# Order of ScalarE's and VectorE's work in the recurrence layer of a seven-block model on one core

## The reference

```python
def rglru_block(xn, w_in, conv_w, conv_b, w_a, b_a, w_x, b_x, lam, w_out):
    u = xn @ w_in
    xb, gate = jnp.split(u, 2, axis=-1)
    xc = lax.conv_general_dilated(xb, conv_w, ...) + conv_b          # 4 taps along time
    r = sigmoid(einsum('bsgi,gij->bsgj', xg, w_a) + b_a)             # 8 blocks of 256
    i_gate = sigmoid(einsum('bsgi,gij->bsgj', xg, w_x) + b_x)
    log_a = -8 * r * softplus(-lam)
    a, bt = exp(log_a), sqrt(-expm1(2 * log_a)) * (i_gate * xc)
    h_t = a_t * h_(t-1) + bt_t                                       # scan along time
    return (h * silu(gate)) @ w_out
```

## Time and profile before

| What | Before |
|---|---|
| Median of 3 runs | 3548.23 us (3548.18 to 3550.38) |
| The profiled execution's own time | 3549.42 us |
| Its span in the profile | 3547.6 us |
| TensorE busy (matmuls) | 3447.0 us, 97% |
| VectorE busy | 2783.1 us, 78% |
| ScalarE busy | 1987.5 us, 56% |
| POOL busy | 587.2 us, 17% |
| Mean granted TensorE clock | 0.995 of full |

### The profile page before, as it was taken

One profiled execution on the slowest core, in us unless ns is written; L12 is line 12 of the kernel. 1 busy time (PEld: TensorE's weight loads), 2 busy tenths in 40 slices (PEclk: granted clock), 3 DMA queues, 4 the chain that ended last, 5 costly groups with the idle time before them and its releaser, 6 DMA issues.

```text
span 3547.6 us, 68240 instructions
## 1 busy us (share of the span) xinstructions
PE 3447.0 (97%) x27858; PEld 3381.8 (95%) x27858; DVE 2783.1 (78%) x4529; ACT 1987.5 (56%) x3204; POOL 587.2 (17%) x546
## 2 busy tenths in 40 slices
PE   7999999999999999999999999999999998999997
PEld 7999999999999998999999999999999998999997
DVE  7788888577797887877888887898989867666665
ACT  6555546566547676565555546665656746434344
POOL 2111112111113011131111112231313300000000
PEclk9999999999999999999999999999999999999999
DMA  6555556444465444655555565556464543555552
GB/s 239 217 197 219 217 227 231 176 155 179 165 251 203 172 169 173 267 185 218 201 221 202 208 262 180 178 175 230 171 233 169 186 169 146 210 189 199 204 190 107
DMA packets 113688, 699.61 MB, mean 197 GB/s; under 512 B 13216, under 2 KB 29792, under 8 KB 31456
## 3 DMA queue, kind: packets, MB, share of 16 engines
q1 hardware_dynamic: 104128, 685.14, 52.2%
q10 hardware_dynamic: 8784, 8.46, 1.0%
q0 software_dynamic: 464, 1.64, 0.1%
HBM read 684.64 MB, written 2.16 MB: 194 GB/s over the span
## 4 chain that ended last, share of the span: by engine, by line
PE 49%; DVE 13%; ACT 6%; issue 2%; DMA 1%; POOL 1%; DVEq 0%; SPq 0%; POOLq 0%; ACTq 0%
PE g L446 15%; PE g L448 15%; PE g L447 15%; DVE w_lo L1594 4%; ACT w_hi L1026 2%; DMA w_raw<-in_slots 1%; POOL scratch L2409 1%; DVE vec L2095 1%; DVE rstd L2095 1%; PE turn_bank L485 1%; DVE scratch L1659 1%; DVE scratch L2121 0%; DVE scratch L2129 0%; PE norm_bank L459 0%; DVE h L2225 0%
## 5 line engine op out<-in xcount | busy, mean ns | idle before, releaser
L1594 DVE TENSOR_TENSOR w_lo<-w_raw,w_hi 128x1024 fp32r<-128x1024 f32 x1088 | 1337.0, 1232 | 433.9 <-ACT w_hi L1026 423.1
L1026 ACT ACTIVATE w_hi<-w_raw 128x1024 fp32r<-128x1024 f32 x1088 | 1129.6, 1053 | 873.2 <-PE g L448 761.7
L446 PE MATMUL g<-p_hi,w_hi 128*128 128x256 f32 x4576 | 1318.0, 288 | 36.4 <-DVE w_lo L1594 23.2
L448 PE MATMUL g<-p_hi,w_lo 128*128 128x256 f32 x4576 | 1296.2, 283 | 0.0
L447 PE MATMUL g<-p_lo,w_hi 128*128 128x256 f32 x4576 | 1296.2, 283 | 0.0
L446 PE MATMUL g<-q_hi,w_hi 128*128 128x256 f32 x3408 | 980.0, 288 | 5.7 <-DVE w_lo L1594 2.2
L448 PE MATMUL g<-q_hi,w_lo 128*128 128x256 f32 x3408 | 964.0, 283 | 0.0
L447 PE MATMUL g<-q_lo,w_hi 128*128 128x256 f32 x3408 | 963.8, 283 | 0.0
L446 PEld LDWEIGHTS g<-p_hi,w_hi 128*128 128x128 f32 x4576 | 879.1, 192 | 46.1 <-DVE w_lo L1594 32.7
L447 PEld LDWEIGHTS g<-p_lo,w_hi 128*128 128x128 f32 x4576 | 879.3, 192 | 1.4
L448 PEld LDWEIGHTS g<-p_hi,w_lo 128*128 128x128 f32 x4576 | 879.0, 192 | 0.0
(11 more groups left out here) (445 smaller groups left out, 3929.2 us busy)
## 6 DMA issues: line engine op xcount, KB each, us to landing
w_raw<-in_slots SPq DMA_DIRECT2D x640, 1024.0 KB, 4.9
scratch<-scratch SPq DMA_DIRECT2D x128, 64.0 KB, 4.9
scratch<-s_rows ACTq DMA_DIRECT2D x16, 256.0 KB, 3.4
con<-s_rows ACTq DMA_DIRECT2D x16, 256.0 KB, 5.1
h<-in_x SPq DMA_DIRECT2D x4, 512.0 KB, 6.2
out_h<-h SPq DMA_DIRECT2D x4, 512.0 KB, 2.6
sq<-in_p POOLq DMA_DIRECT2D x4, 256.0 KB, 3.0
con<-in_consts SPq DMA_DIRECT2D x1, 832.0 KB, 10.7
```

The source lines that it names most:

```text
L446: pe.matmul(g, wh, hi[:, k], start=n == 0, stop=False)
L448: last = pe.matmul(g, wl, hi[:, k], start=False, stop=n == len(ks) - 1)
L1026: act.activation(w_hi[k % SPLIT][:, cols], raw[MAIN_AT[k] % RAW][:, cols], ACT.Copy).then_inc(hi_ready, 1)
L1594: dve.tensor_tensor(w_lo[k % SPLIT][:, cols], raw[MAIN_AT[k] % RAW][:, cols], w_hi[k % SPLIT][:, cols], SUB).then_inc(lo_ready, 1)
```

## The change

Two things change, both in the recurrence layer. On ScalarE the block of a z slot (sigmoid of the gate tile, high part of the output tile before it, and in z12 the split of the `ple` input) moves from behind the group's chain to ahead of it; in slots without a piece of a chain nothing changes. On VectorE the four scans of a group are cut in two for groups 1, 2 and 3: the first two stay 5 slots after the group, the other two come at the end of the next slot. Group 0 keeps its four in one slot. No instruction is added or removed.

```diff
@@ -1319,6 +1319,12 @@
                 else:
                     act.wait_ge(tile_done, c.next("tile"))
                 hi_ahead(1)
+                if kind == "z":
+                    sigmoid(c_zc[n % 2], clamped, c.next("clamped"))
+                    if n:
+                        y_high(n - 1)
+                    if n == 12:
+                        split_p(layer)
                 for g in range(4):
                     if s == C_AT[g] + 1:
                         c_sigmoid(rg, 8 * g + 4)
@@ -1328,12 +1334,6 @@
                         c_decay()
                     if s == C_AT[g] + 4:
                         c_scale()
-                if kind == "z":
-                    sigmoid(c_zc[n % 2], clamped, c.next("clamped"))
-                    if n:
-                        y_high(n - 1)
-                    if n == 12:
-                        split_p(layer)
             y_high(DT - 1)
             p_slot()
             out_and_gates(layer, x, y)
@@ -2007,10 +2007,10 @@
                 last = dve.tensor_tensor(b[:, 512 * e:512 * e + 512], b[:, 512 * e:512 * e + 512], bS[e][:], MUL)
             link(last)
 
-        def c_scan(g):
-            for n in range(4):
-                last = dve.tensor_tensor_scan(xc[:, 4 * g + n], rg[:, n], ig[:, n], 0.0, MUL, ADD)
-            link(last)
+        def c_scan(g, first, last):
+            for n in range(first, last):
+                done = dve.tensor_tensor_scan(xc[:, 4 * g + n], rg[:, n], ig[:, n], 0.0, MUL, ADD)
+            link(done)
 
         def layer_c(layer, x, y):
             lam_ = vec[:, VEC["c_lambda"]:VEC["c_lambda"] + DT]
@@ -2066,7 +2066,9 @@
                         c_input_gate(g)
                     if s == C_AT[g] + 5:
                         c_scale()
-                        c_scan(g)
+                        c_scan(g, 0, 2 if g else 4)
+                    if g and s == C_AT[g] + 6:
+                        c_scan(g, 2, 4)
             finish(DT - 1)
             low(DT - 2)
             low(DT - 1)
```

## The result

The kernel after the change takes 3567.07 us, the median of 5 runs (3563.53 to 3568.04), against 3548.18 us for the kernel before in the same comparison (5 runs, 3545.65 to 3550.38). The ratio is 1.0051, with a 95% interval of 1.0040 to 1.0062: slower by some 19 us, half a percent. The forecast was 3567.4.

What follows compares the result with a forecast made beforehand. TensorE, busy 97%, bounds the kernel; in late z slots ScalarE waits for POOL's clamp. Order + 20.4 and scans - 1.2 give + 19.2 us (19.1 slot by slot): 3568.5 profiled, median 3567.4, range 3557 to 3574.

Steps and rivals of the forecast that it cites:

- The chain stands behind the clamp's wait: ScalarE, seven z slots: a group's chain would wait for POOL's clamp instead of filling that time, 20.4 us lost.
- The terms: Loss per z slot with a chain piece (13, 20, 22, 25 to 28): 2.6 to 3.2 us each, sum 20.4.
- The scans: VectorE, two of four scans one slot later: 1.2 us gained in group 3, 0 in groups 1 and 2.
- Passing on: Between the seven slots: each delay arrives in full; TensorE's slots 19 to 22 only some 2 us later.
- The earlier high part: VectorE's wait for the high part (L1309): serving it earlier frees 0, at most 0.4 us a slot.
- The clock: TensorE's gaps before slots 25 and 28 to 31: falls to the lower clock level there cost 0.
- The signs: Expected in the later profile: seven new ScalarE waits for POOL of 2.3 to 3.2 us, slots 26 to 28 longer.
- the test: TensorE's slot 32, at 1357.22 before: forecast wrong if it starts less than 15 us later.
- absorption of the early slots: ScalarE's waits for TensorE between z1 and z2 make slots 13 and 20 cost nothing: 3561 us, chance 0.08.
- Slack on TensorE all along: TensorE keeps the slack of slots 19 to 22 throughout, so the time does not change; chance 0.04.
- A lasting low clock: TensorE at the lower clock level from slot 28 to 31: some 3 us more, 3570.5 us, chance 0.08.
- the scans decide: Seven z slots wait under 0.5 us for the clamp, three scan splits win 1.22 us each: median 3544.6, chance 0.04.

Runs made afterwards that it cites:

- the order alone: ScalarE's new order (sigmoid and high part ahead of the chain) with VectorE's scans unsplit, against the kernel before: 3568.24 us, ratio 1.0057.
- the halves: Two kernels, ScalarE's new order only in slots 13, 20, 22 or only in 25 to 28, scans unsplit, against the kernel before: 3557.41 and 3558.88 us.
- the high part alone: Only the high part moved ahead of the chain, sigmoid left behind it, scans unsplit, against the kernel before: 3569.40 us, ratio 1.0059.

## Why the prediction was right

It gave 3567.4 us with a range of 3557 to 3574, and 0.92 for slower; the median is 3567.07. That the two agree to 0.3 us is luck: the interval of the ratio leaves 14 to 22 us for the loss, and the two profiled executions differ by 16.8 us in span. What carries the account is the single slots, which the traces show to a few hundredths. Going by the prediction's own steps:

- **The chain stands behind the clamp's wait, and the hole that it filled is lost.** Shown by the order alone (+20.30), the halves (9.11 + 11.17), and the high part alone (+20.46), in which another wait of the same kind does the same.
- **The terms.** Forecast 3.18, 3.18 and 3.2 for slots 13, 20 and 25: measured 3.11, 3.12 and 3.11. Forecast 2.8 for slot 22: 2.89. Forecast 2.7, 2.6 and 2.7 for slots 26 to 28: 2.70, 2.68, 2.69. Their sum is 20.30 against 20.4. A further 0.25 us comes up before the slots 20 and 25; it is the scans' (next point).
- **The scans** give 1.18 in group 3 (forecast 1.2). In groups 1 and 2 I put them at 0, and they cost 0.11 and 0.14. TensorE's gap only moved from slot 26 to 27.
- **Passing on.** It passes on in full, as forecast, and TensorE starts slots 19 to 22 by 1.93 to 2.02 us later (forecast some 2), slot 23 by 4.54. Two readings on the way were wrong, without a price. In slots 23 and 24 ScalarE is not without idle time: it waits 2.58 us for the clamp and then 4.10 for the gate reads (L1989), and the delay goes on over VectorE, whose gate reads of slot 25 come 9.37 us later. And of ScalarE's 6.6 us of waiting for TensorE only two waits, 4.8 us, lie between z1 and z2.
- **The earlier high part gives back 0.** From the start of ScalarE's first half to VectorE's (L1594) it is 1.15 us in slot 29 before (1346.52 to 1347.67) and 1.16 in slot 28 after (1356.51 to 1357.67), so nothing is won. The reading behind it was off: what happens 0.3 us ahead of T is the start of the high part. VectorE's wait for it ends 0.13 us behind T, at 1346.65, and it then still waits 0.59 for the half.
- **The clock.** I put its falls at 0, and the Trainium skill (TensorE: Matmul & The Clock Gate, "Why this matters for your kernels") warns that idle gaps between bursts of matmuls send the clock back to half. The trace agrees with it that the clock falls after gaps, of 4.5 and 5.1 us among others. Its price is nil in this place. The slot that starts at 1359.38 runs at the lower level at first, and TensorE still waits 2.71 us for the take behind it. The gaps that I forecast before slots 28 to 31 (3.4 to 5 us) came out as 3.58, 1.76, 5.06 and 2.71, because slow matmuls filled part of them.
- **The signs.** The waits of ScalarE for POOL grew in seven slots, five of them new and two lengthened, as forecast. That each would last 2.3 to 3.2 us missed two: 3.54 in slot 20, where the former 0.41 is in it, and 7.25 in slot 25, where I had not counted that the chain's wait for L1989 would merge with it. No time hangs on either. The slot times of 9.3, 10.9 and 10.5 are 9.23, 11.03 and 10.55. TensorE begins slot 32 without a gap at 1377.24, 20.0 us later than at 1357.22 and over the 15 that I had put as the test. The take that it needs was at 1376.04, so by the 0.56 us of before it could have begun at 1376.6: the last low spell holds it up by 0.6 us here, and the clamps behind show nothing of it (19.37 to 19.39).

The rivals: absorption of the early slots would have given 6.4 us less, and slots 13 and 20 cost 3.12 and 3.11 with nothing else moved but slot 22. Slack on TensorE all along would have given nothing. A lasting low clock would have added 3, and nothing of it is there. For "the scans decide" the waits would have to be under 0.5 us; the smallest new one is 2.58.

Why ScalarE can't use the hole otherwise is in its queue's order: the path in a z slot is weight half, take, clamp, sigmoid, next weight half, over three engines, and ScalarE has 2.58 us in the middle of it that only work without a wait can fill.

## What to carry to other kernels

Before moving an instruction forward in the queue of an in-order engine, look for what waits it carries and what it would be moved past: work that waits for nothing hides in another's wait if it stands ahead of it (here 2.6 to 3.1 us each time) and is paid in full behind it. If one engine's wait for another shows in every pass of a loop (here 2.58 us in the plain slots), the move that helps is the other one, back by a pass, behind work that the next pass needs anyway; here it took the time from 3548.0 to 3542.6 where the forward move took it to 3567. And a wait that one sees on a second engine (17.0 us of VectorE at L2039) is no reason to serve it sooner, as long as that engine then waits for the same first engine anyway.

## What the runs showed of the hardware that I had not expected

The same instruction on POOL has different durations. A clamp of 128x256 float32 takes 1.65 us in most z slots, and 0.84 to 0.91 when repeated right behind itself, as shown above. The kernel before has both as well, in clamps behind the layer (timeline of POOL):

```profile
1492.97 1.64 POOL L2409 TENSOR_SCALAR scratch<-scratch 128x256 f32<-128x256 f32 x1 [7.71 <-DVE scratch L1702]
1498.77 0.85 POOL L2409 TENSOR_SCALAR scratch<-scratch 128x256 f32<-128x256 f32 x1 [4.16 <-DVE scratch L1702]
...
1503.84 1.89 POOL L2409 TENSOR_SCALAR scratch<-scratch 128x256 f32<-128x256 f32 x1 [3.34 <-DVE scratch L1702]
...
1509.89 0.85 POOL L2409 TENSOR_SCALAR scratch<-scratch 128x256 f32<-128x256 f32 x1 [3.46 <-DVE scratch L1702]
```

The two-input work of VectorE next to them decides, as far as the rows go. Timeline of VectorE around the same four clamps:

```profile
1492.69 1.22 DVE L1594 TENSOR_TENSOR w_lo<-w_raw,w_hi 128x1024 fp32r<-128x1024 f32 x1
...
1498.80 1.45 DVE L1594 TENSOR_TENSOR w_lo<-w_raw,w_hi 128x1024 fp32r<-128x1024 f32 x1 [0.22 <-ACT w_hi L1026]
...
1503.80 1.23 DVE L1594 TENSOR_TENSOR w_lo<-w_raw,w_hi 128x1024 fp32r<-128x1024 f32 x1 [0.15 <-ACT w_hi L1026]
1504.94 0.62 DVE L1666 SCALAR_TENSOR_TENSOR q_lo<-h,vec,q_hi 128x256 fp32r<-128x256 f32 x1
...
1509.91 1.46 DVE L1594 TENSOR_TENSOR w_lo<-w_raw,w_hi 128x1024 fp32r<-128x1024 f32 x1 [0.21 <-ACT w_hi L1026]
```

Where the weight half (L1594, two inputs from SBUF) starts first, at 1492.69 and 1503.80, the clamp lasts until 0.8 us after its end (1492.69 + 1.14 to the next start = 1493.83, and the clamp ends at 1494.61; 1504.94 and 1505.73). Where the clamp starts first, by 0.02 or 0.03 us, it takes 0.85 and the weight half 1.45 instead of 1.23. In a plain z slot the second half starts some 0.28 us before the clamp (1356.99 and 1357.27 in slot 30 of the kernel before), and the clamp takes 1.65. The Trainium skill (SBUF — State Buffer, "SBUF: two separate sides") says that a VectorE instruction with two SBUF inputs and a POOL instruction that reads SBUF share one pair of ports, and that whichever starts first has it for the whole instruction and the other blocks. These rows agree where the half is first; where the clamp is first the half loses 0.22 us and not the clamp's 0.85. No run tested it, so the cause is not shown. If it holds, a z slot in which VectorE lets the clamp start ahead of its second half would have the sigmoid some 0.8 us sooner.

The other thing is how little the clock's fall can matter. The clock fell in five spells, three of them in slots 28, 30 and 31, and the terms of slots 26 to 28 came out at 2.70, 2.68 and 2.69 us, as worked out without any fall (2.7, 2.6 and 2.7). TensorE was waiting for the next take there anyway. The last spell, in slot 31, showed in TensorE's own start of slot 32, by 0.6 us, and in no clamp.
